# A hybrid delta-rule, stick-breaking and mixture-of-experts block: weighted sums made transposed on column halves

## What is computed

```
h = rms_norm(x, ln_mix);  proj = h @ w_in  -> qkv, z, b, a (delta rule), q, k, v (stick breaking)
# gated delta rule, 4 heads of 128, chunk by chunk, state per head:
v_new = u - w @ state
o     = (q * exp(gc)) @ state + qk @ v_new
state = state * exp(g_last) + (k * exp(g_last - gc)).T @ v_new
gdn   = rms_norm(o, gdn_norm_w) * silu(z)
# stick-breaking attention, 8 heads of 64, for blocks of 128 tokens:
weights = exp(log_sigmoid(logits) + sum of log_sigmoid(-logits) after s), causal
att     = rms_norm(weights @ v, sb_norm_w)            # over the 64 features of a head
x = x + concat(gdn, att) @ w_out
x = x + hierarchical_moe(rms_norm(x, ln_moe))         # 64 experts, 2 per token
x = x + sigmoid(rms_norm(x, ln_ple) @ w_gate) * (p @ w_proj);  out = rms_norm(x, ln_final)
```

## Time and profile before

| | us |
|---|---|
| median of three runs | 1546.78 |
| lowest and highest | 1546.55, 1548.45 |
| the profiled execution | 1548.61 |
| its span, first to last instruction | 1546.6 |

### The profile page before, as it was taken

One profiled execution on the slowest core, in us unless ns is written; L12 is line 12 of the kernel. 1 busy time (PEld: TensorE's weight loads), 2 busy tenths in 40 slices (PEclk: granted clock), 3 DMA queues, 4 the chain that ended last, 5 costly groups with the idle time before them and its releaser, 6 DMA issues. The chain is left out here.

```text
span 1546.6 us, 16490 instructions
## 1 busy us (share of the span) xinstructions
PE 1383.3 (89%) x5986; PEld 743.0 (48%) x5986; DVE 553.6 (36%) x847; ACT 358.9 (23%) x674; POOL 257.5 (17%) x372
## 2 busy tenths in 40 slices
PE   6999999999999999999999687788778878789997
PEld 4445864444458878874555232232223323234443
DVE  3323024432227887872455221211211111124543
ACT  2221132100036666651212101000000100004322
POOL 1000000110014544532110111111111111111110
PEclk8999999999999999999999899999989999999999
DMA  5212025743422220106214499999999999982231
GB/s 195 68 68 69 14 70 170 196 116 89 141 104 62 65 73 28 29 8 272 81 63 150 173 411 420 421 420 417 418 411 399 404 403 403 402 368 91 82 122 41
DMA packets 107879, 306.96 MB, mean 198 GB/s; under 512 B 22560, under 2 KB 61360, under 8 KB 82096
## 3 DMA queue, kind: packets, MB, share of 16 engines
q1 hardware_dynamic: 98032, 289.42, 49.0%
q0 software_dynamic: 9792, 16.80, 2.9%
HBM read 285.16 MB, written 39.90 MB: 210 GB/s over the span
## 5 line engine op out<-in xcount | busy, mean ns | idle before, releaser
L1620 PE MATMUL pe_gu<-w_gu,xT 128*64 128x512 f32 x1024 | 266.8, 681 | 97.1 <-DMA w_gu<-in_w_expert_up 91.2
L251 PE MATMUL ps<-wide,gst 128*128 128x512 f32 x640 | 285.7, 607 | 3.2 <-DVE wide L404 3.2
L1620 PEld LDWEIGHTS pe_gu<-w_gu,xT 128*64 128x64 f32 x1024 | 82.2, 155 | 259.8 <-issue 257.9
L251 PEld LDWEIGHTS ps<-wide,gst 128*128 128x128 f32 x640 | 123.6, 195 | 155.1 <-issue 153.3
L1824 DVE TENSOR_TENSOR hs<-sg,pe_gu 128x256 f32<-128x256 f32 x32 | 13.5, 421 | 361.0 <-ACT sg L1736 361.0
L1314 PE MATMUL p_x<-wide,pw 128*128 128x512 f32 x256 | 116.4, 608 | 2.1 <-DVE mx L1174 1.4
L1638 PE MATMUL pe_y<-wide,hTe 128*64 128x512 f32 x512 | 115.4, 592 | 1.1 <-DVE ys L1829 1.1
L901 POOL TENSOR_TENSOR wt<-brk,Pm 128x512 f32<-128x512 f32 (+3 forms) x96 | 91.1, 950 | 125.1 <-DVE Pm L827 120.7
L265 PE MATMUL psk<-w_tok,wide 128*128 128x260 f32 (+1 forms) x384 | 111.7, 453 | 0.0
L1709 PE MATMUL pe_y<-w_gu,xT 128*128 128x512 f32 x256 | 111.2, 592 | 0.0
L1560 POOL DMA_INDIRECT y_d<-ys,row_at x32 | 32.5, 1017 | 425.8 <-DVE ys L1829 415.1
(11 more groups left out here) (303 smaller groups left out, 1572.7 us busy)
## 6 DMA issues: line engine op xcount, KB each, us to landing
w_gu<-in_w_expert_gate SPq DMA_DIRECT2D x64, 1024.0 KB, 11.8
w_gu<-in_w_expert_up SPq DMA_DIRECT2D x64, 1024.0 KB, 16.5
wide<-in_w_expert_down SPq DMA_DIRECT2D x64, 1024.0 KB, 19.6
gst<-in_w_in SPq DMA_DIRECT2D x20, 512.0 KB, 4.0
wide_tab<-y_d SPq DMA_DIRECT2D x8, 1024.0 KB, 5.6
qkv_d<-y_sb SPq DMA_DIRECT2D x12, 512.0 KB, 2.6
qk_st<-rows_d SPq DMA_DIRECT2D x8, 768.0 KB, 9.6
gst<-qkv_d SPq DMA_DIRECT2D x8, 768.0 KB, 4.8
```

Source lines behind the costliest of these rows:

```text
L251: last = pe.matmul(ps[s][:, c], w_ct[:, s, k, :], hT[:, k, c], start=k == 0, stop=k == KT - 1)
L1620: last = pe.matmul(p_gu[e * CAP:(e + 1) * CAP, :], xT[:, s, k, e * CAP:(e + 1) * CAP], wv[:, e, :, k, :], start=k == 0, stop=k == KT - 1)
```

## The change

Seven things change; the first three belong together.

1. **Weighted sums with values stationary, on column halves.** The stationary operand is now v_sb, 128 keys by the 64 features of one head, the moving one wT, 128 columns of query tokens. Head e = 0 of a pair goes to partitions 0 to 63 of OB, head e = 1 to 64 to 127. weighted(m) handles a pair of strips in one call, block by block with the two heads in turn, and is called every second step, for strips g-4 and g-3. wT holds two pairs. So OB, and the attention's part of mx, have features on the partitions and tokens in columns.
2. **The output projection takes them so.** turn_s and copy_s go. The sums of squares per token now lie across partitions: head_sums multiplies the squares (stationary, 128 by 128) with of_head, two columns of zeros and ones, into p_ss. VectorE makes mean and EPS of it (mean_squares). The factors are brought back across the partitions by head_factors: eight matmuls with a column of mss, broadcast to 64 columns, as the stationary operand and the identity as the moving one, into p_rs on column halves. norm_heads multiplies mx with p_rs and writes into mT.
3. **Places in the steps.** head_sums(t+1) stands ahead of project(s, 0, 0) in steps 1 to 6, and waits for msq_ok, the squares of tile t+1, and for m_ok. In step 0, head_factors(0) and head_sums(1) stand between the two halves of the product. head_factors(t+1) stands behind turn_g(t+1). On VectorE norm_heads(t+1) moves behind choose(t-2), and norm_heads(1) behind gated_last.
4. **The state in one fused pass per head**: St = St * col_last + GA, four operations; Sg and the piece gain go.
5. **The norm in one fused pass per head** in place of two passes over all four.
6. **scale_w_o moves from VectorE to ScalarE**, at positions 14 and 22 of a round.
7. **Room and loads**: nsq lies in w_r, own in ln_row. So w_r is loaded after the last nss_ok, and ln_row after the last scan. TensorE waits for the setup only at its first ks.

```diff
-        ACT_AT = {"y1": 0, "xq": 2, "square": 4, "y2": 9, "vn": 18}
-        DVE_AT = {"scale0": 0, "q": 1, "gain": 1, "x": 2, "v": 3, "sum": 3, "k": 5, "xT": 6, "r": 7, "scale1": 8, "norm": 9, "s": 10, "o": 11}
+        ACT_AT = {"y1": 0, "xq": 2, "square": 4, "y2": 9, "scale0": 14, "vn": 18, "scale1": 22}
+        DVE_AT = {"q": 1, "x": 2, "v": 3, "sum": 3, "k": 5, "xT": 6, "r": 7, "norm": 9, "s": 10, "o": 11}
...
-                def weighted(g):
-                    t, n, c0, c1, e = at(g)
+                def weighted(m):
+                    g = 2 * m
+                    t, n, c0, c1, _ = at(g)
                     if g % NS == 0:
                         reach(pe, at_done, g // NS)
-                    pe.wait_ge(ev_done, g + 1)
...
-                    for b in range(m):
-                        last = pe.matmul(OB[:, n, e * SD:(e + 1) * SD], wT[:, e, b * P:(b + 1) * P], v_sb[:, c0 // P + b, h * SD:(h + 1) * SD],
+                    pe.wait_ge(ev_done, g + 2)
+                    nb = (c1 - c0) // P
+                    for b in range(nb):
+                        for e in range(2):
+                            h = g // (2 * NS) * 2 + e
+                            last = pe.matmul(OB[e * SD:(e + 1) * SD, n, :], v_sb[:, c0 // P + b, h * SD:(h + 1) * SD], wT[:, m % 2, e, b * P:(b + 1) * P],
...
-                    if g >= 3:
-                        weighted(g - 3)
+                    if g >= 4 and g % 2 == 0:
+                        weighted(g // 2 - 2)
...
-                        dve.wait_ge(Sg_ok, i + 1)
-                        dve.tensor_tensor(St[:], Sg[:], GA[:], ALU.add).then_inc(S_ok, 1)
+                        for h in range(GH):
+                            last = dve.scalar_tensor_tensor(St[:, h, :], St[:, h, :], col_last[:, i * GH + h:i * GH + h + 1], GA[:, h, :], ALU.mult, ALU.add)
+                        last.then_inc(S_ok, 1)
...
+                def head_sums(t):
+                    pe.wait_ge(msq_ok, t + 1)
+                    if t:
+                        pe.wait_ge(m_ok, t)
+                    for k in range(HK):
+                        last = pe.matmul(p_ss[:, 2 * k:2 * k + 2], msq[:, t % 2, k * P:k * P + P], of_head[:], start=True, stop=True)
+                    last.then_inc(ms_sum, 1)
+                def head_factors(t):
+                    pe.wait_ge(ms_ok, t + 1)
+                    for h in range(SH):
+                        last = pe.matmul(p_rs[h % 2 * SD:(h % 2 + 1) * SD, h // 2, :], mss[:, t % 2, h:h + 1].to_broadcast([P, SD]), ident[:],
+                                         start=True, stop=True)
+                    last.then_inc(rs_done, 1)
...
                     if not first:
                         pe.wait_ge(x_ok, t)
+                    if not first and not last:
+                        head_sums(t + 1)
                     project(s, 0, 0)
                     project(s, 0, 1)
                     if first:
-                        turn_s(0, True)
+                        head_factors(0)
+                        head_sums(1)
                     else:
                         h_transposes(t - 1, 1 - s)
                     if not last:
...
                         turn_g(t + 1, False)
-                        turn_s(t + 1, False)
-                    pe.wait_ge(sT_ok, t + 1)
+                        head_factors(t + 1)
+                    pe.wait_ge(m_ok, t + 1)
                     project(s, HK, 0)
```

More of the change, by code:

```diff
@@ L622, in _ @@
                     load_z(i + 2)
+                sp.wait_ge(nss_ok, NT - 1)
+                sp.dma_start(w_r[:, :, 0:NG], A["w_router_group"][0].rearrange("(p k) c -> p k c", k=KT)).then_inc(small_in, 16)
+                sp.dma_start(w_r[:, :, NG:NG + NE], A["w_router_expert"][0].rearrange("(p k) c -> p k c", k=KT)).then_inc(small_in, 16)
+                sp.wait_ge(scan_done, G)
+                sp.dma_start(ln_row[:], A["ln_moe"][0:1, :].to_broadcast([P, D])).then_inc(small_in, 16)
             @block.tensor
@@ L774, in attended, with scale_w_o @@
                         act.activation(mx[:, 3:6, c], OB[:, 1:4], ACT.Copy).then_inc(at_done, 1)
+                def scale_w_o(k):
+                    act.wait_ge(wo_in, 16)
+                    act.wait_ge(nw_in, 48)
+                    last = act.activation(w_o[:, k, :], w_o[:, k, :], ACT.Copy, scale=nw[:, k // GH:k // GH + 1])
+                    if k == KT - 1:
+                        last.then_inc(wo_ok, 1)
                 def delta(piece, i):
+                    if piece[0:5] == "scale" and 1 <= i <= KT // 2:
+                        scale_w_o(2 * (i - 1) + int(piece[5]))
                     if piece[0] == "y":
@@ L1162, in _, with mean_squares @@
             def _(dve):
[L1163 to L1165 removed]
+                def mean_squares(t, s):
+                    dve.wait_ge(ms_sum, t + 1)
+                    dve.tensor_scalar(mss[:, s], p_ss, 1.0 / SD, EPS, ALU.mult, ALU.add).then_inc(ms_step, 1)
                 def norm_heads(t, s):
[L1168 to L1169 removed]
+                    dve.wait_ge(rs_done, t + 1)
+                    dve.tensor_tensor(mT[:, s, HK:], row(t, slice(GW, None)).rearrange("p (k n) -> p k n", k=HK), p_rs, ALU.mult).then_inc(m_ok, 1)
                 def add_to_x(t, s, n):
@@ L1274, in _ @@
                         choose(t - 2)
+                    norm_heads(t + 1, 1 - t % 2)
                     add_to_x(t, t % 2, t // 2)
@@ L1302, in turn_g @@
                     last.then_inc(gtr_done, 1)
-                def turn_s(t, first):
-                    pe.wait_ge(m_ok, t + 1)
-                    if not first:
-                        pe.wait_ge(sT_ok, t)
-                    for k in range(HK, KT):
-                        last = pe.transpose(p_m[:, k, :], row(t, slice(k * P, k * P + P)), ident[:])
-                    last.then_inc(str_done, 1)
+                def head_sums(t):
[11 more added lines that the diff above has]
+                    last.then_inc(rs_done, 1)
                 def project(s, k0, h):
@@ L1380, in _ @@
                 turn_g(0, True)
+                pe.wait_ge(head_ok, 4)
+                head_sums(0)
                 for t in range(NT):
```

88 lines of the change are left out of this document (32 added, 56 removed).

## The result

The changed kernel takes 1570.0 us in the median of four executions (1563.1 to 1573.2), the kernel before 1546.7 beside it: ratio 1.0143, 95% interval 1.0107 to 1.0179. The execution that was profiled took 1563.05 us for a span of 1561.3 us, the one of before 1548.61 and 1546.6, so what the profile can explain is +14.4 to +14.7 us. It is the fastest of the four. The change makes the kernel slower, by 0.8 to 0.9% in those two and by 1.4% in the first.

A forecast was written before the change was run, and what follows sets the result against it. TensorE's program order was taken to set the time of mixers and output projection. Mixers -20.7, steps 1 to 6 +19.3, step 0 +5.6 and clock +8.5 summed to +12.7 us: 1559 us, range 1538 to 1573.

The forecast's parts named there:

- Weighted sums: Mixers: 288 pairs at 112 ns plus 48 visits at 0.35 us; saving 15.4 us, between -3 and 32.
- OB's wait: Mixers: TensorE's waits for ScalarE's copies of bank OB, 6.8 us, go.
- New waits in the mixers: Mixers: 1.5 us charged for new waits, bounds 0 and 8.
- if that cover were gone: Mixers: VectorE's work beside TensorE costs 0; uncovered, the fused update would delay S_ok by 3 us.
- The slack at the chain's end: Mixers: GpSimd's product ended 1.3 us before its transpose began, read as slack.
- Rival E: Mixers become bound by the chain through ScalarE, VectorE and GpSimd; new waits eat about 12 us: 1571 us; chance 0.12.
- Steps 1 to 6: Output projection: 6 x (1.5 idle + 0.9 + 1.25 - 0.44) = 19.3 us longer.
- Step 0: Output projection: its first step has no neighbour to hide in and gets 5.6 us longer (3 to 7).
- The clock: Output projection: four of seven places fall to half clock, some twice as long; 8.5 us (0 to 20).
- B: Output projection: the clock holds, so the sum is +4.2 us: 1551 us; chance 0.20.
- C: Mixers and projection: visits to column halves are free, so the sum is -7 us: 1540 us; chance 0.20.
- D: Mixers and projection: short records on column halves do not overlap, +52 us: 1599 us; chance 0.06.

The follow-up runs named there:

- e0: The changed kernel again, no edit: 1557.3 us, ratio 1.0080; its repetition 1558.5 us, ratio 1.0087.
- e7: e1 with the two loops of weighted() exchanged, all blocks of one head before the other: 1555.3 us, ratio 1.0070.
- e5: e1 with the state's update in two passes again (Sg and the gain come back): 1546.5 us, ratio 1.0007.
- e9: e5 with output step 0 reordered, and the weighted sums and ScalarE's copy of OB one step later: 1545.9 us, ratio 1.0006.
- e1: The changed kernel with head_sums(t+1) behind project(s, 0, 0) instead of in front, in steps 1 to 6: 1545.4 us, ratio 0.9987.
- e8: e1 with a TensorE wait for ScalarE's squares added in front of project(s, 0, 0) in output steps 1 to 6: 1553.8 us, ratio 1.0054.
- e4: The mixers of before with the new output stage, output values not the block's: 1581.8 us, ratio 1.0254.
- e2: The changed kernel with two 512-column products that nobody reads in front of head_sums in steps 1 to 6: 1554.6 us, ratio 1.0062.

## Why the prediction was right, and where it was not

The forecast was 1559 us, +12.7 on the sum. The profiled executions differ by 14.4 us, the two later medians by 11 and 12; the first median, 1570, is inside the range by 3 us. Its excess of some 12 us over the other two is clock (the product of span and clock is the same), and no term of the sum had foreseen it. The mechanism was right: work is saved in the mixers, and more than that is lost in the output stage to new records, one new wait and the clock. That the total comes so near is luck in part. In e0's trace the mixers gave 4.8 us less than foretold, and the output stage cost 4.3 us less than its 33.4; the two errors cancel. Without the clock's term the sum was +4.2; mixers and output less their clock losses are +6.9.

**Weighted sums: right.** Foretold were 32.3 us for 288 pairs and 0.35 us for each of 48 visits, a saving of 15.4. Pairs and visits are seen at those prices, and TensorE's busy time in the mixers fell by 17.3. e7 shows what the pairing hangs on. The Trainium skill, "TensorEngine Tiling (Array Packing)", Key Properties, has the array drain when the tiling mode changes, and its table Theoretical Speedup promises up to 2x for halves. The trace is in line with both: 1.03 us instead of 1.79 inside a visit, and a third of that gain given back around it (0.23 of 0.76; the 0.13 inside is already taken off). That the price of a visit is a drain, no run shows.

**OB's wait: right.** The copies of OB (L771 and L774, now L775 to L779) are in no wait of TensorE in the changed kernel.

**New waits in the mixers: the mis-sized term.** I charged 1.5 us, with a bound of 8. The waits other than those for OB's copies went from 5.3 to 12.8 us, +7.5. Two of them make 8.1: the sigmoid (4.5), which I had not named because I looked only at the chain's end, the transposes; and the fused update (3.6, where the state's sum of before had 0.4), which I had priced at 3 "if that cover were gone", and then put at nothing since VectorE works beside TensorE. It does, but S_ok is where the two meet. e5 takes 2.2 of it back. So the mixers gave 15.9 to 16.3 us and not 20.7.

The slack at the chain's end was read wrongly too. The 1.3 us between GpSimd's product and its transpose at 550.70 hold a wait that the change was about to remove, and that the earlier trace rows leave out:

```profile
549.24 0.66 PE L655 MATMUL OB<-v_sb,wT 128*128 128x64 f32 x4 [1.11 <-ACT mx L771]
```

Without those 1.1 us some 0.2 are left, by this estimate. That this hand-off stayed on time all the same (the wait for wt went from 1.2 to 1.4 us) was luck; e9 moves the sums by one step and it takes 5.7.

Rival E, mixers bound by the chain, came true in part. New waits ate 7.5 of the 22.2 us that the sums and OB's wait were to give, a third, where E had a third to two thirds and 12 us. Its sign, idle time behind GpSimd's wt, did not come: the waits are for ScalarE and VectorE. The shares of before misled me: a stage that gets 17 us of TensorE's work taken out is nearer to its other engines than they say.

**Steps 1 to 6: right.** Foretold 19.3 us. From the first add_to_x to the seventh it was 103.9 us before and is 130.5; less 6.8 for the clock that makes +19.7. The first and the seventh, before and then after:

```profile
715.59 1.22 DVE L1174 TENSOR_TENSOR mx<-pw,p_x 128x1024 f32<-128x1024 f32 x1 [9.45 <-PE p_x L1314]
819.51 1.22 DVE L1174 TENSOR_TENSOR mx<-pw,p_x 128x1024 f32<-128x1024 f32 x1 [4.75 <-PE p_x L1314]
704.94 1.22 DVE L1171 TENSOR_TENSOR mx<-pw,p_x 128x1024 f32<-128x1024 f32 x1 [6.47 <-PE p_x L1322]
835.40 1.22 DVE L1171 TENSOR_TENSOR mx<-pw,p_x 128x1024 f32<-128x1024 f32 x1 [6.37 <-PE p_x L1322]
```

The idle time, foretold as 9.0, is 10.3, but 1.4 of it, at step 1, was there before. The records alone, foretold at 10.3, are e1's steps: 114.0 us, +10.1. This was the prediction's best step, and it came from one place: laying the new wait against start times of an old step, one row under the other. Eight records with two columns took 0.88 us, as L258's row said. The Trainium skill, same page, Instruction Overhead, has some 60 cycles for a very short matmul; no run here shows so little where each record brings a full stationary load.

**Step 0: right within its bounds.** From the stage's first record to the first add_to_x it was 20.3 us and is 26.4; less 3.4 and 5.1 for the clock that is +4.4, where 5.6 had been foretold. The 5.6 is itself a slip: its terms, 0.9 + 1.25 + 0.69 + 0.85 + 0.9 + 1.7 + 1.25 - 1.2, add up to 6.3, and with that the sum would have been +13.4. The rest of the stage, behind the last of the six steps, got 1.5 us shorter in that measure, which nothing had foretold.

**The clock: right in size by luck, loosely in mechanism.** Foretold were 8.5 us, from a guess of four falls in seven places. The stage lost 9.9 us more than before in the first trace, 6.2 and 6.4 in the two others. In steps 1 to 6 three of six places fell in the first trace and two in each of the others, and step 0 got one fall of 3.4 us more than before. The row I leaned on, 1.6 us of work in 3.4 and then a fall, was a fair picture of the 3.2 us wait (TensorE was busy for 1.18 us from 705.90 to 709.30); of the short waits most did nothing. I had taken the wait and the short records as one cause. e8 parts them, and the long wait is enough by itself.

**The rivals.** B (clock holds) falls with the windows, C (free visits) with the timeline around a visit, D with 1.03 us for sixteen records. E is answered above.

## What to carry to other kernels

Before a wait is put in front of an engine that sets the pace, lay its source's start time against the engine's next work in a trace of the old kernel: here one call, moved behind 3.5 us of work that was ready, was worth 12 us, as much as the whole loss. Where a change takes much work off the bounding engine, take out of the slack that you read every wait that the change removes, and look at every hand-off of its loop and not only at the one the change touches. A fused pass that saves an engine time can still cost some, if it moves work from before a dependency to behind it. And where executions of one kernel differ by 10 us, set their mean clocks beside their spans before looking for a reason in the code.

## What the runs showed of the hardware

- Whether records on two column halves overlap depends on how far apart in the program they stand: 16 records of 128 columns took 1.03 us in turn and 1.51 us in two runs of eight, and would take 1.79 us at the 112 ns of a record on the full array. Eight records took 0.60 us either way.
- A wait of TensorE of 3.1 to 3.3 us, with the engine busy before and after, was followed by 3.4 us at 0.50 (1.2 GHz) in each of the five traces that have it (the changed kernel, e0 and its repetition, e4, e8). The twenty-five waits of 1.3 to 1.5 us behind it in the same traces were followed by a fall four times.
- With work whose result nobody reads in place of idle time, the stage without its clock loss stayed the same (186.5 us beside 186.0) and no fall came in the steps where it stood, in one trace (e2).
- VectorE's fused operation on 128x128 took 0.33 us in the state's update, which reads one tensor from PSUM, and 0.69 us in the norm, whose tensors all lie in SBUF. Why is not shown.
- The front, whose code is the same everywhere, held between 3.4 and 23.9 us at 0.50 and took 442.9 to 451.8 us. Single executions of one kernel differ by 7 to 19 us of some 1550, and the mean granted clock goes with most of it: within a measurement the span scattered by 2.6 to 6.5 us (standard deviation), the span times the clock by 0.4 to 2.1.
